# A hybrid attention and expert layer on one core: the first gated-attention operands are fetched and split during stick-breaking attention, the slot table is computed in three pieces earlier in the expert loop, and the last stage's normalization is rearranged

## The reference

```
u = rmsnorm(x) @ w_in                    # columns: sq sk sv | gq gk gv glr gr | mq | gates
sb  = stick_breaking(sq, sk, sv)         # 8 heads x 64
la  = log_sigmoid(glr @ w_gla_a2 + b_gla_a) / 16        # glr has 16 columns
gla = gated_linear_attention(gq / 8, gk, gv, la)        # 4 heads, 64-row chunks
gla = rmsnorm_per_head(gla) * gla_norm * silu(gr)
mem = softmax cross attention of mq on 256 memory rows
h   = x + (sum_b sigmoid(gate_b) * (o_b @ w_branch[b])) @ w_out
idx, wts = route(rmsnorm(h))             # group of 8 experts, then the top 2 of them
y   = rmsnorm(h + wts0*expert[idx0] + wts1*expert[idx1]) * norm_final
```

## Time and profile before

| what | value |
|---|---|
| median of 3 runs | 1905.25 us |
| the profiled execution: its own time, its span | 1906.05 us, 1904.5 us |
| TensorE busy, share of the span | 1778.7 us, 93% |
| VectorE busy | 1054.4 us, 55% |
| ScalarE busy | 866.0 us, 45% |
| GpSimd busy | 121.9 us, 6% |
| HBM read, written | 286.08 MB, 39.87 MB |

### The profile page before, as it was taken

The page is one execution under the profiler, slowest core; times in us unless marked ns, Lnnn a source line. Parts: engine busy times, 40 slices in busy tenths (PEclk is TensorE's granted clock), DMA queues, the critical chain, the costliest instruction groups (busy, mean ns, idle before and its releaser), DMA issues. The chain is left out here.

```text
span 1904.5 us, 25559 instructions
## 1 busy us (share of the span) xinstructions
PE 1778.7 (93%) x10344; PEld 1564.6 (82%) x10344; DVE 1054.4 (55%) x1291; ACT 866.0 (45%) x1112; POOL 121.9 (6%) x136
## 2 busy tenths in 40 slices
PE   7999999899999999999999999969999999999960
PEld 5887777788898879999999998848888888888850
DVE  4326555333245432133243155568888889889857
ACT  4224554323263331121122223247878878878832
POOL 0013000000000021000000000000010000010003
PEclk9999999899999999999999999979999999999985
DMA  5231110202012226111112142169999999999947
GB/s 177 84 103 39 29 29 1 58 23 71 23 42 78 73 60 209 39 45 51 42 42 94 29 172 89 50 248 367 418 415 416 412 415 415 412 413 418 406 149 271
DMA packets 139179, 329.86 MB, mean 173 GB/s; under 512 B 13659, under 2 KB 91319, under 8 KB 114358
## 3 DMA queue, kind: packets, MB, share of 16 engines
q1 hardware_dynamic: 123556, 272.69, 38.7%
q0 software_dynamic: 10896, 38.74, 5.6%
q10 hardware_dynamic: 4608, 16.78, 2.2%
HBM read 286.08 MB, written 39.87 MB: 171 GB/s over the span
## 5 line engine op out<-in xcount | busy, mean ns | idle before, releaser
L2362 DVE TENSOR_TENSOR low<-raw,hig 128x2048 fp32r<-128x2048 f32 x192 | 431.6, 2285 | 68.2 <-ACT hig L2131 67.6
L2131 ACT ACTIVATE hig<-raw 128x2048 fp32r<-128x2048 f32 x192 | 359.4, 1915 | 23.1 <-ACT ye L2202 14.5
L1984 PE MATMUL bank<-hig,xel 128*128 128x512 f32 x512 | 204.3, 399 | 3.9 <-DVE xel L2429 3.9
L1986 PE MATMUL bank<-hig,xeh 128*128 128x512 f32 x512 | 201.1, 393 | 0.0
L1985 PE MATMUL bank<-low,xeh 128*128 128x512 f32 x512 | 200.8, 392 | 0.0
L71 PE MATMUL bank<-xhi,glo 128*128 128x384 f32 (+1 forms) x552 | 180.1, 326 | 3.6 <-ACT sg L2084 2.2
L73 PE MATMUL bank<-xhi,ghi 128*128 128x384 f32 (+1 forms) x552 | 180.0, 326 | 0.0
L72 PE MATMUL bank<-xlo,ghi 128*128 128x384 f32 (+1 forms) x552 | 179.9, 326 | 0.0
L71 PE MATMUL gproj<-xhi,glo 128*128 128x384 f32 (+1 forms) x408 | 142.4, 349 | 3.0 <-DVE glo L1350 3.0
L72 PE MATMUL gproj<-xlo,ghi 128*128 128x384 f32 (+1 forms) x408 | 137.3, 337 | 0.0
L73 PE MATMUL gproj<-xhi,ghi 128*128 128x384 f32 (+1 forms) x408 | 137.0, 336 | 0.0
(11 more groups left out here) (408 smaller groups left out, 3505.6 us busy)
## 6 DMA issues: line engine op xcount, KB each, us to landing
raw<-in_w_e_gate_dram SPq DMA_DIRECT2D x64, 1024.0 KB, 7.8
raw<-in_w_e_up_dram SPq DMA_DIRECT2D x64, 1024.0 KB, 8.2
raw<-in_w_e_down_dram SPq DMA_DIRECT2D x64, 1024.0 KB, 7.5
graw<-in_w_in_dram SPq DMA_DIRECT2D x40, 512.0 KB, 3.8
expert_rows<-ye ACTq DMA_DIRECT2D x32, 512.0 KB, 8.0
xt<-in_x_prompt_dram SPq DMA_DIRECT2D x16, 512.0 KB, 3.7
expert_rows<-nil POOLq DMA_DIRECT2D x16, 512.0 KB, 10.3
braw<-in_w_branch_dram SPq DMA_DIRECT2D x24, 256.0 KB, 2.8
```

The source lines that it names most:

```text
L1984: nc.tensor.matmul(bank[:, :], xel[n % 2][:, kk, :], wh[:, k, :], start=(kk == 0), stop=False)
L1986: last = nc.tensor.matmul(bank[:, :], xeh[n % 2][:, kk, :], wh[:, k, :], start=False, stop=(kk == KC - 1))
L2131: nc.scalar.activation(hig[q % HI][:, :], raw[q % RAW][:, :], ACT.Copy).then_inc(high, 1)
L2362: nc.vector.tensor_tensor(low[q % RAW][:, :], raw[q % RAW][:, :], hig[q % HI][:, :].bitcast(F32), ALU.subtract).then_inc(lowed, 1)
```

## The change

1. `w2c`, `bat`, `gnt` and their three semaphores are made at the start, in places of their own. SyncE loads them at the end of stage 1's list, and a sixth block `q_load(5)` (the first gated-attention query columns) follows, once `query(4, 2)` is done. `q_split(5)` is done in the last round of stage 1 on ScalarE and on VectorE. In stage 2, units 0 to 2 use `whq` and `wlq`; the loads start with block 1, and block 3 waits for nothing.
2. `slots()` is cut into `overflow()`, `order()` and `slots()`. They run at the end of the iterations 8, 11 and 14 of VectorE's expert loop.
3. In stage 4 `1/sqrt(mean + eps)` is `exp(-0.5 * ln(mean + eps))`, both on ScalarE directly after the square; the table set is loaded at the stage's start. VectorE keeps three operations a tile. There are nine `yo` buffers, so no wait for a store.

The core of the diff:

```diff
-                c0 = C_SQ + b * P if b < HW else C_LR
+                c0 = C_SQ + b * P if b < HW else C_LR if b == HW else C_GQ
...
             sp.wait_ge(vstored, 16 * NT)
+            for p in range(2):
+                sp.dma_start(w2c[p][:, :], io["w_gla_a2"][0, :, p * P:(p + 1) * P]).then_inc(w2_in, 16)
+            with nc.allow_non_contiguous_dma(reason="a few hundred scalars, once"):
+                sp.dma_start(bat[:, :], io["b_gla_a"][0, :].rearrange("(h p) -> p h", p=P)).then_inc(biases, 16)
+                sp.dma_start(gnt[:, :], io["gla_norm"][0, :].rearrange("(h p) -> p h", p=P)).then_inc(gains, 16)
+            q_load(HW + 1)
...
-                if t < NR and i == SSTEP and hp + 2 <= HW:
+                if t < NR and i == SSTEP and hp + 2 <= HW + 1:
                     q_split(hp + 2)
...
-                if b >= 3:
+                if b > 3:
                     sp.wait_ge(projected, done[b - 3])
...
-            for b in range(3):
+            for b in range(1, 4):
                 load(b)
...
-                pe.wait_ge(g_low, b + 1)
+                wh, wl = (ghi[b % 2], glo[b % 3]) if b else (whq, wlq)
+                if b:
+                    pe.wait_ge(g_low, b)
...
-            w_high(0)
             w_high(1)
             softplus(0)
...
-            w_low(0)
             w_low(1)
...
-                    if n == NE - 1:
-                        slots()
                     multiply(n)
                 if n + 1 < NE:
                     x_low(n + 1)
                 if 0 < n < NE:
                     split_low(q0 + 8)
                     split_low(q0 + 9)
+                if n in (8, 11, 14):
+                    (overflow, order, slots)[(n - 8) // 3]()
...
+            nc.scalar.preload_act_table_set("natural_log_exp_and_others")
             for t in range(NT):
-                r = rows_of(t)
+                R = slice(0, rows_of(t))
                 act.wait_ge(summed, t + 1)
-                nc.scalar.activation(junk[0:r, :], ya[t][0:r, :], ACT.Square, scale=D ** -0.5,
-                                     accum_out=stat[0:r, t:t + 1]).then_inc(sq_done, 1)
-                act.wait_ge(inverted, t + 1)
-                nc.scalar.activation(stat[0:r, 32 + t:33 + t], stat[0:r, 16 + t:17 + t], ACT.Sqrt).then_inc(rooted, 1)
+                nc.scalar.activation(junk[R, :], ya[t][R, :], ACT.Square, scale=D ** -0.5, accum_out=stat[R, t:t + 1])
+                act.drain()
+                nc.scalar.activation(stat[R, 16 + t:17 + t], stat[R, t:t + 1], ACT.Ln, bias=eps[R, :])
+                act.drain()
+                nc.scalar.activation(stat[R, 32 + t:33 + t], stat[R, 16 + t:17 + t], ACT.Exp, scale=-0.5).then_inc(rooted, 1)
...
-                ve.wait_ge(sq_done, t + 1)
-                nc.vector.tensor_scalar(stat[0:r, 16 + t:17 + t], stat[0:r, t:t + 1], EPS, None, ALU.add)
-                ve.drain()
-                nc.vector.reciprocal(stat[0:r, 16 + t:17 + t], stat[0:r, 16 + t:17 + t]).then_inc(inverted, 1)
                 ve.wait_ge(rooted, t + 1)
-                if t >= 3:
-                    ve.wait_ge(os_[t % 3], 16 * (t // 3))
-                nc.vector.scalar_tensor_tensor(out=yo[t % 3][0:r, :], in0=ya[t][0:r, :], scalar=stat[0:r, 32 + t:33 + t],
+                nc.vector.scalar_tensor_tensor(out=yo[t][0:r, :], in0=ya[t][0:r, :], scalar=stat[0:r, 32 + t:33 + t],
```

More of the change, by code:

```diff
@@ L158, in build @@
     identb = at("identb", [P, P], BF16, CON + 2944)
+    w2c = [at("w2c", [RANK, P], F32, CON - 1024 + 512 * p) for p in range(2)]
+    bat = at("bat", [P, 2], F32, R2 + 49664)
+    gnt = at("gnt", [P, 4], F32, R2 + 49696)
+    w2_in, biases, gains = [nc.alloc_semaphore(name=f"gl_{n}") for n in ("w2_in", "biases", "gains")]
     ORDER = ["d", 7, 0, 6, 1, 5, 2, 4, 3]
@@ L865, in _ @@
         def _(sp):
[L866 to L869, removed]
             def load(b):
@@ L887, in states_out @@
                 sp.dma_start(gouts[p * P:(p + 1) * P, :], S[:, 18, :]).then_inc(stored, 16)
-            for b in range(3):
+            for b in range(1, 4):
                 load(b)
-            with nc.allow_non_contiguous_dma(reason="a few hundred scalars, once"):
-                sp.dma_start(gnt[:, :], io["gla_norm"][0, :].rearrange("(h p) -> p h", p=P)).then_inc(gains, 16)
             sp.wait_ge(consts, 1)
             state_in(0)
-            for b in range(3, 9):
+            for b in range(4, 9):
                 load(b)
@@ L966, in unit @@
                 three_pass(nc, half(pj2, j % 2)[:, 0:n], [
-                    (ghi[b % 2][:, k, :], glo[b % 3][:, k, :], high(k), low(k)) for k in range(KC)]).then_inc(projected, 1)
+                    (wh[:, k, :], wl[:, k, :], high(k), low(k)) for k in range(KC)]).then_inc(projected, 1)
             def turn(p, kind, g):
@@ L2476, in slots @@
                 nc.vector.tensor_scalar(isov[:, :, :], rk[:, :, :], float(MAIN), None, ALU.is_ge)
-                ve.drain()
+            def slots():
                 for k in range(2):
@@ L2529, in build @@
     yb = [at("yb", [P, D], F32, OS + 8192 * i + 4096) for i in range(NT)]
[L2530 to L2533, removed]
+    yo = [at("yo", [P, D], F32, 4096 * i) for i in range(NT)]
+    gf = at("gf", [P, D], F32, 36864)
+    junk = at("junk", [P, D], F32, 40960)
     with Stage(nc) as ctx:
-        g_in, summed, sq_done, inverted, rooted, finished, o0, o1, o2_, *ys_ = sems(
-            ctx, "z", "g_in summed sq_done inverted rooted finished o0 o1 o2 " + " ".join(f"y{t}" for t in range(NT)))
-        os_ = [o0, o1, o2_]
+        g_in, summed, rooted, finished, stored, *ys_ = sems(
+            ctx, "z", "g_in summed rooted finished stored " + " ".join(f"y{t}" for t in range(NT)))
         block = ctx.enter_context(nc.Block())
@@ L2547, in _ @@
                 sp.wait_ge(finished, t + 1)
[L2548 to L2551, removed]
+                sp.dma_start(yp[t * P:t * P + r, :] if t < FULL else ysm[:, :], yo[t][0:r, :]).then_inc(stored, 16)
+            sp.wait_ge(stored, 16 * NT)
         @block.gpsimd
```

16 lines of the change are left out of this document (7 added, 9 removed).

## The result

The changed kernel takes 1887.28 us (median of 4 executions, 1886.41 to 1888.70), the kernel before 1905.58 us in the executions beside it. The ratio on record is 0.9897 with a 95% interval of 0.9881 to 0.9913. Against the 1905.25 us of the forecast that is 1885.6 us: faster, as forecast, by 19.7 us where 13.9 were, and beyond the fast end of the range, 1887.2. The quotient of the two medians is 0.9904, which would be 1887.0 us; the miss is a small one by either figure. The profiled execution took 1887.47 us, 18.6 less than that of before. One execution of the kernel before, of 2266.84 us at a granted clock of 0.742, is left out of every comparison here.

The account below looks back on a forecast made before the run. TensorE, busy 93% of the span, was taken as the bound, with transfers also full in the expert loop. Terms -5.6 - 3.7 - 0.6 - 4.0 = -13.9 us gave 1891.4 us, range 1887.2 to 1897.0.

Parts of the forecast that it names:

- the clock term: Clock gains at the edits: 1.2 us at stage 2's start (0 to 2.8), 0.6 at the last expert (0 to 1.6).
- The rest of stage 2 keeps it: Stage 2 after its start: the gain stays, as TensorE has no idle time over 0.5 us from 361 to 400.
- Start of stage 2: Low-rank product starts at once, first projection 5.6 us earlier; a shorter low-clock fall gives another 1.2 us.
- the gate chain: ScalarE and VectorE work at stage 2's start, 13.4 us; claimed in time by 0.2 us, nothing charged.
- unit 4: Stage 2 TensorE work needing unit 2's drain: due at 356.1, drain done at 355.9, so no wait.
- The tail: End of stage 1: VectorE's low-part copy ahead of the `collect` delays the rest by 1.2 us (0.9 to 2.2).
- The slot table: Off VectorE's path at the last expert: last `down` 3.7 us earlier; its pieces in the expert loop cost 0.
- The clock term of 0.6: Last expert's `down`: a shorter idle time ahead may avoid the low clock, gain 0 to 1.6 us, 0.6 taken.
- Rival (d): Expert loop: the pieces break its rhythm, each of 17 later experts takes longer; at 1.2 us each 1911.8 us; chance 0.04.
- The last stage: Stage 4: VectorE takes 3.76 us a tile, not 4.41; gain 4.0 us, between 2.9 and 5.1.
- the wait of 2.2 us for tile 7's `yb`: Stage 4: earlier stores delay this gather, tile 7 at 1887.7 instead of 1885.5, cutting the gain from 5.1 to 2.9.

Follow-up runs that it names:

- part 2 alone: Only the slot table's split into three pieces at iterations 8, 11 and 14, against the kernel before; 1901.61 us, ratio 0.9974.
- kernel in one piece: Changed kernel with the whole slot table in one piece at the end of iteration 8; 1890.21 us, ratio 0.9910.
- kept busy: Changed kernel with 16 more unread 128x512 TensorE products in idle times between the last tile's routing and the first expert; 1887.72 us, ratio 0.9900.
- Part 3 alone: Only the last stage's three VectorE operations a tile, against the kernel before; 1902.05 us, ratio 0.9974.

## Why the prediction fell short

**The step that failed** is the clock term: "The gain is between 0 and 2.8; I take 1.2" and "gain 0 to 1.6, I take 0.6". Both are bounds of the clock at the edits, and the sum had no term for it elsewhere; instead it said "The rest of stage 2 keeps it: TensorE's list follows without an idle time over 0.5 us from 361 to 400". The list does follow, but the clock of its work doesn't stay. Between 364 and 1289 us it was worth -6.4 us in the first trace of the changed kernel, nothing in the second and -6.8 in the third. The second low-rank product showed it in the forecast's own rows: 0.50 with dense work on both sides. I read there that this product doesn't hold the clock up, and not that such stretches, far from the edits, could come and go. A term of 0 with bounds of some 6 us on either side would have given 1881 to 1903.

**Start of stage 2.** The beginning was right: the low-rank product 1.50 us behind TensorE's last work, and the stage's loads, the gate chain and unit 4 as said. Of -5.6 and -1.2 the trace gave -5.2 in all, because the product ran at the low clock, 3.8 us for the 2.2 taken; the second execution of the same kernel had the 2.2 and an offset lower by 3.2 us.

**The tail** cost 1.13 us for 1.2, and the copy moved behind the `collect` took it away.

**The slot table** gave 3.76 us for 3.7, and its three pieces cost nothing. The clock term of 0.6 was 1.4; part 2 alone had 1.5. Rival (d) is refuted by the kernel in one piece: a slip of 3.0 us stays 3.0.

**The last stage** gave 5.2 us for 4.0, the second term that was off. VectorE's own 3.76 us a tile held. What failed is the wait of 2.2 us for tile 7's `yb`, half of which was charged. Counted from the stage's first gather issue, that gather landed at 33.2 us in the trace that the forecast was read from, and at 31.6, 31.9 and 32.8 in the three others with the old last stage; in the changed kernel it landed at 31.7, and the tile's addition was due at 32.25. It did hold VectorE up in two other kernels with the new stage, by 0.17 us (table in one piece) and 0.49 (kept busy, the line below):

```profile
1873.77 1.29 DVE L2587 SCALAR_TENSOR_TENSOR ya<-ya,wts,mixT 128x1024 f32<-128x1024 f32 x1 [0.49 <-DMA yb<-expert_rows,sidx]
```

From issue to landing this one gather took as long as before (11.9 us, 12.1 in the earlier trace rows), but its neighbours took longer: from `yb` of tile 5 to `yb` of tile 8 the others took 0.5 to 1.5 us more. They were also issued earlier in the stage, so that the first four of them landed within 0.2 us of where they had, and the last two 0.2 and 1.1 us sooner. The earlier issue comes from GpSimd: of the fifteen issues ahead of tile 7's `yb` one took over 1.5 us (1.76), where before the change three had (1.55 to 1.58); the same goes for all four traces with the old last stage (three) and all ten with the new one (at most one). So it belongs to the new order of VectorE's work; by which way was not tried. The Trainium skill (DMA: Bandwidth & Descriptors, Queues, rings and completion order) says that each DMA engine goes round-robin between its queues, a packet at a time. Whether the stores or their own earlier issue made the neighbours slower, no run here tells; the 2.2 us that the forecast had drawn from that rule did not come. Part 3 alone, with the old rest, gives -5.1.

**Sum.** At the places -14.5 for -13.9. The forecast was nearly right there because its errors cancel (stage 2 by +1.6, last stage by -1.2, last expert's clock by -0.8), and wrong in what it left out.

**Open.** Whether the missing 4 us are luck of the changed kernel's timing or of these executions. The mean of its 14 executions is 18.7 us below that of the 49 of before, 4.2 more than the places give in the first trace, with a standard error of 0.7 us, so it favours a lasting part; and 1.2 us of delay takes it away (mean 12.7 below the kernel before, with one of 1.3). That fits an outcome set by when the work of stage 2 falls in time, but no run here shows what it is counted from. The Trainium skill (TensorE: Matmul & The Clock Gate, Part 1: The HAM clock gate) says that the activity is watched in a rhythm that doesn't start with the kernel, and that the number of slow products therefore varies from run to run. The traces agree: two executions of one kernel, 32.3 and 19.9 us of low-clock work. The same section puts the penalty of the clock's ramp under 1% of a typical span and advises against fitting a count of slow products; here the two executions differ by some 6 us of 1888, 0.3%, a third of the gain to be forecast.

## What to carry to other kernels

A forecast from one profiled execution should list every low-clock stretch of the whole span, and not only those at the edit: of those behind a short stop many, though not all, can go or come with a shift in time, or with none, and the range needs that sum on both sides. A gain or cost under about 5 us in a kernel like this is read from the offset between two traces at its place, not from a median of four executions. Cover is a matter of piece size: the same 7.3 us of VectorE work cost 3.0 us in one piece and nothing in three.

## What the runs showed of the hardware

A stop of about 1.5 us (TensorE busy for 0.08 and 0.49 of two microseconds) is followed by 0, 3.4 or 6.8 us at 1.2 GHz in different executions. Executions of one kernel spread by up to 11 us on a single core, with some 1.9 us for 0.001 of the mean granted clock. Sixteen unread products of 128x512 kept the clock at 1.00 over 24 us that otherwise ran at 0.50, and saved 2.1 us there, where half of the 9.4 us of work in that stretch is 4.7. Where the output stores came earlier and closer together, the last gathers took 0.5 to 1.5 us more from issue to landing, except one (11.9 us for 12.1). Issues of an indirect transfer by GpSimd mostly took 0.95 us, and now and then 1.5 to 1.9: three of the first fifteen beside five VectorE operations a tile, at most one beside three.
